# Sweeping the first weight pair of a sublayer by high and low parts, an earlier norm of half A, and x updates ahead of low parts

## The reference, cut to what matters

```python
def rmsnorm(x, g):
    y = xf * lax.rsqrt(jnp.mean(xf * xf, axis=-1, keepdims=True) + EPS)
    return (y * g.astype(jnp.float32)).astype(x.dtype)
def ffn_half(x, g_pre, g_post, w_gu, w_dn):
    return x + 0.5 * rmsnorm(swiglu(rmsnorm(x, g_pre), w_gu, w_dn), g_post)
...
    x = ffn_half(x, g[0], g[1], w_ffn_gu[l, 0], w_ffn_dn[l, 0])
    u = rmsnorm(x, g[2])      # u @ w_in, two attentions, then @ w_out
    x = x + rmsnorm(mix, g[3])
    qc = (rmsnorm(x, g[4]) @ w_cq[l])
    x = x + rmsnorm(oc, g[5])
    x = ffn_half(x, g[6], g[7], w_ffn_gu[l, 1], w_ffn_dn[l, 1])
```

## Time and profile before

| | us |
|---|---|
| median of 3 runs | 2788.9 (2785.92 to 2790.43) |
| the profiled execution, its own time | 2787.24 |
| its span, first to last instruction | 2785.4 |
| PE busy | 2610.1 (94%) |
| DVE busy | 1272.3 (46%) |
| ACT busy | 900.8 (32%) |

### The profile page before, as it was taken

The page is one execution under the profiler, slowest core; times in us unless marked ns, Lnnn a source line. Parts: engine busy times, 40 slices in busy tenths (PEclk is TensorE's granted clock), DMA queues, the critical chain, the costliest instruction groups (busy, mean ns, idle before and its releaser), DMA issues.

```text
span 2785.4 us, 48225 instructions
## 1 busy us (share of the span) xinstructions
PE 2610.1 (94%) x19513; PEld 2471.8 (89%) x19513; DVE 1272.3 (46%) x2307; ACT 900.8 (32%) x1576; POOL 67.9 (2%) x199
## 2 busy tenths in 40 slices
PE   7999998999898889999989999989898988999998
PEld 6999998986587789999989999989755977999998
DVE  4444325345846554442254442253457555444323
ACT  3222223224533432222232222232344534322221
POOL 1000000001100000000000000000111000000000
PEclk9999999999989999999999999999998998999999
DMA  5233332330023023233223233233310321223321
GB/s 178 85 88 90 91 91 86 116 120 25 24 91 105 18 68 90 84 95 94 67 69 88 85 92 93 73 101 116 105 40 31 92 75 31 83 83 90 97 84 64
DMA packets 383972, 229.81 MB, mean 83 GB/s; under 512 B 6636, under 2 KB 371198, under 8 KB 383840
## 3 DMA queue, kind: packets, MB, share of 16 engines
q1 hardware_dynamic: 378272, 206.59, 25.3%
q0 software_dynamic: 4368, 16.92, 1.7%
q10 hardware_dynamic: 1200, 4.46, 0.4%
HBM read 214.39 MB, written 18.79 MB: 84 GB/s over the span
## 4 chain that ended last, share of the span: by engine, by line
PE 83%; DVE 11%; ACT 2%; issue 2%; DMA 1%; DVEq 0%; SPq 0%; ACTq 0%
PE psum L607 73%; PE psum L810 3%; PE psum L582 3%; PE psum L829 2%; DVE u_lo L1280 2%; DVE w_lo L1285 2%; DVE x L1326 1%; DVE probs L1469 1%; PE psum L622 1%; DVE y_ffn L1320 1%; DVE y_mix L1320 1%; ACT w_hi L993 1%; PE psum L823 1%; PE psum L831 0%; DMA w_raw<-in_w_ffn_gu 0%
## 5 line engine op out<-in xcount | busy, mean ns | idle before, releaser
L607 PE MATMUL psum<-u_hi,w_hi 128*128 128x272 f32 x4096 | 906.8, 295 | 62.1 <-DVE w_lo L1285 24.2
L607 PE MATMUL psum<-u_hi,w_lo 128*128 128x272 f32 x4096 | 894.3, 292 | 0.0
L607 PE MATMUL psum<-u_lo,w_hi 128*128 128x272 f32 x4096 | 892.3, 292 | 0.0
L607 PEld LDWEIGHTS psum<-u_hi,w_hi 128*128 128x128 f32 x4096 | 671.7, 193 | 72.8 <-DVE u_lo L1280 28.3
L993 ACT ACTIVATE w_hi<-w_raw 128x1024 fp32r<-128x1024 f32 (+1 forms) x336 | 376.8, 1121 | 1105.6 <-PE psum L607 1091.2
L607 PEld LDWEIGHTS psum<-u_lo,w_hi 128*128 128x128 f32 x4096 | 672.5, 193 | 0.0
L607 PEld LDWEIGHTS psum<-u_hi,w_lo 128*128 128x128 f32 x4096 | 667.9, 193 | 0.0
L1285 DVE TENSOR_TENSOR w_lo<-w_raw,w_hi 128x1024 fp32r<-128x1024 f32 (+1 forms) x336 | 436.5, 1299 | 348.3 <-ACT w_hi L993 348.3
L607 PE MATMUL psum<-h_hi,w_hi 128*128 128x272 f32 x1408 | 305.7, 288 | 0.5
L607 PE MATMUL psum<-h_lo,w_hi 128*128 128x272 f32 x1408 | 304.5, 287 | 0.0
L607 PE MATMUL psum<-h_hi,w_lo 128*128 128x272 f32 x1408 | 304.4, 287 | 0.0
(11 more groups left out here) (189 smaller groups left out, 2097.1 us busy)
## 6 DMA issues: line engine op xcount, KB each, us to landing
w_raw<-in_w_ffn_gu SPq DMA_DIRECT2D x176, 512.0 KB, 3.8
w_raw<-in_w_ffn_dn SPq DMA_DIRECT2D x64, 704.0 KB, 4.6
w_raw<-in_w_in SPq DMA_DIRECT2D x48, 512.0 KB, 3.7
w_raw<-in_w_out SPq DMA_DIRECT2D x16, 512.0 KB, 3.9
w_raw<-in_w_ckv SPq DMA_DIRECT2D x16, 512.0 KB, 3.8
bias_tab_dram<-bias_rev_dram POOLq DMA_DIRECT2D x1, 5120.0 KB, 21.3
table<-bias_tab_dram SPq DMA_DIRECT2D x16, 320.0 KB, 2.9
out<-k_nat POOLq DMA_DIRECT2D x4, 1024.0 KB, 5.0
```

The costliest lines, as they stand in the source:

```text
L607: pe_last[0] = pe.matmul(psum[:, bank + part, 0:c1 - c0], w, xx[:, c0:c1], start=s0, stop=s1)
```

## The change

PE's `first_chunks` no longer runs the three products of a block together. It makes sweeps over all eight blocks with one kind of product: for half A, high x high and then high activation x low weight for slot 0, the same for slot 1 (with half B's spread of y between the two), then the low activations of slot 0 and of slot 1; for half B, slot 0's and slot 1's sweeps likewise, with the low activations of slot 0 ahead of slot 1's low weights. Each matmul of a sweep waits for its own block. In the last output tile of a feed-forward sublayer, half A's norm comes before the fifth of the eleven blocks of half B's first part (slot 0), and its spread before the ninth, both in the same part; before, the norm stood behind that part and the spread in the second. ACT makes slot 1's `w_hi` after the last two high parts of half A and not before them. DVE does all four y and x steps of a half and then the eight low parts, with slot 1's low weights after the fourth. `sum_x` is split: `fold_x` does its first addition, and `late_sums` puts the low weights between the fold and the rest.

Eight low parts stand there now between the two copies; before there were two. The diff, cut to its core:

```diff
-            half_chunk(pair, 0, 0, u_in, range(KD), 0, True, True, arrived(0))
-            if between:
-                between()
-            half_chunk(pair, 1, 2, u_in, range(KD), 0, True, True)
-            half_chunk(pair, 0, 0, u_in, range(KD), 1, True, True, arrived(1)).then_inc(chunk_done, 1)
-            half_chunk(pair, 1, 2, u_in, range(KD), 1, True, True).then_inc(chunk_done, 1)
+            def sweep(slot, bank, half, weight, part, first=False, last=False):
+                for k in range(KD):
+                    u = (u_hi, u_lo)[part]
+                    pe.wait_ge((u_hi_ready, u_lo_ready)[part], 16 * q + 8 * half + k + 1)
+                    if first and half == 0 and slot == 0 and k == 4 and norm_late:
+                        norm_late()
+                    pe_last[0] = pe.matmul(psum[:, bank + half, 0:H], weight[:, slot, k * 128:(k + 1) * 128],
+                                           u[:, k, half * H:half * H + H], start=first and k == 0, stop=last and k == KD - 1)
+                return pe_last[0]
+            pe.wait_ge(w_hi_ready, 2 * pair + 1)
+            sweep(0, 0, 0, w_hi, 0, first=True)
+            pe.wait_ge(w_lo_ready, 2 * pair + 1)
+            sweep(0, 0, 0, w_lo, 0)
+            pe.wait_ge(w_hi_ready, 2 * pair + 2)
+            sweep(1, 2, 0, w_hi, 0, first=True)
+            if spread_late:
+                spread_late()
+            pe.wait_ge(w_lo_ready, 2 * pair + 2)
+            sweep(1, 2, 0, w_lo, 0)
+            sweep(0, 0, 0, w_hi, 1, last=True)
+            sweep(1, 2, 0, w_hi, 1, last=True)
+            sweep(0, 0, 1, w_hi, 0, first=True)
+            sweep(0, 0, 1, w_lo, 0)
+            sweep(1, 2, 1, w_hi, 0, first=True)
+            sweep(0, 0, 1, w_hi, 1, last=True).then_inc(chunk_done, 1)
+            sweep(1, 2, 1, w_lo, 0)
+            sweep(1, 2, 1, w_hi, 1, last=True).then_inc(chunk_done, 1)
...
-            half_chunk(pair, 0, 2, h_in, range(DNB), 1, True, False).then_inc(chunk_done, 1)
-            norm_y(l, st, 0)
             def early(k):
-                if k == DNB + 5:
+                if k == 4:
+                    norm_y(l, st, 0)
+                if k == 8:
                     spread_y(l, st, 0)
-            half_chunk(pair, 1, 2, h_in, range(DNB, KF), 1, False, True, early).then_inc(chunk_done, 1)
+            half_chunk(pair, 0, 2, h_in, range(DNB), 1, True, False, early).then_inc(chunk_done, 1)
+            half_chunk(pair, 1, 2, h_in, range(DNB, KF), 1, False, True).then_inc(chunk_done, 1)
...
             root_late()
-            cut_second()
             for k in range(6, KD):
                 high(q, 0, k, gain)
+            cut_second()
...
-                if p and gain is not None:
-                    low(q, half, 2 * p - 2, gain)
-                    low(q, half, 2 * p - 1, gain)
...
-                low(q, half, KD - 2, gain)
-                low(q, half, KD - 1, gain)
+                for k in range(KD):
+                    low(q, half, k, gain)
+                    if later:
+                        later(k)
...
+            fold_x(q, 0)
+            cut_lo(pair + 1, 0)
             sum_x(q, 0)
-            cut_lo(pair + 1, 0)
+            fold_x(q, 1)
+            cut_lo(pair + 1, 1)
             sum_x(q, 1)
-            cut_lo(pair + 1, 1)
```

30 lines of the change are left out of this document (16 added, 14 removed).

## The result

| | before | after |
|---|---|---|
| median of the first 4 runs of each, us | 2787.41 (2784.29 to 2790.43) | 2768.33 (2765.27 to 2771.31) |
| the profiled execution, its own time | 2787.24 | 2765.27 |
| its span | 2785.4 | 2763.5 |
| granted clock over the span | 0.968 | 0.972 |

Five more runs gave 2768.44.

A forecast was written before the change was run, and what follows sets the result against it. PE bounds the kernel (busy 94% of the span), so only places where it waits or runs slowly count; 4.3 + 3.4 + 3.2 + 1.6 - 4.6 - 0.2 = 7.7 us gained, median 2781.2, range 2769.5 to 2789.

The forecast's parts named there:

- FFN handover: Handover where half B's update starts 5.8 us earlier and the tail behind it loses 1.5: 4.3 us gained.
- two IN handovers: Handovers timed to the next norm of x: gain 2.8 us, less 1.1 for another clock fall; 3.4 for two.
- two CO handovers: Handovers with half A's norm unmoved: half B starts 2.2 us earlier, the tail loses 0.6; 3.2 for two.
- end of the program: At the program's end, half B's update starts at 2766.5 instead of 2768.14, and the output follows: 1.6 us gained.
- in front of cross-attention, two: Ahead of cross-attention, DVE's block of eight low parts and waits for weights make PE 2.3 us later; 4.6 for two layers.
- long runs: Stretches of 2844 back-to-back matmuls, 357.75 us, 0.126 each: claimed unable to get shorter, so no gain counted.
- rival 1: In PE's sweeps, each met wait costs up to 0.10 us more per matmul, 488 matmuls, 49 us: 2830; chance 9%.
- what half B's start waits for: In IN and FFN handovers, DVE: PE's spread is done at 442.4, before DVE is free at 443.6; 5.8 us earlier.
- the tail at the lower clock: Behind half B's start, 24 matmuls at 0.227 us: next pair at +14.6, IN norm at +19.1 (full clock +12.3, +16.9).
- The charge of 1.1: In each IN handover, 1.1 us for the chance of another clock fall after PE's idle 2.3 us.
- rival 2: PE keeps its full clock through the handovers' sparse stretches: 19.4 us gained, 2769.5; chance 13%.
- rival 3: In the handovers the tail eats the head through more clock falls and later weights: 0.9 us gained, 2788; chance 18%.

The follow-up runs named there:

- after_all_fill: The changed kernel plus matmuls with unread results where PE idles in and behind handovers and ahead of the four long runs; 2769.74 us.
- early_norm_only: The kernel before with only half A's earlier norm and spread, at three handovers behind a feed-forward sublayer and at the end; 2775.31 us.

## Why the prediction was too small

The change gains 19.1 us by the medians and 21.0 by the two pairs of spans; the sum had 7.7 on six kinds of places. By the marks of two traces each:

| step of the prediction | forecast gain | measured |
|---|---|---|
| FFN handover | 4.3 | 5.5 |
| two IN handovers | 3.4 | 6.0 |
| two CO handovers | 3.2 | 5.2 |
| end of the program | 1.6 | 1.7 |
| in front of cross-attention, two | -4.6 | -4.7 |
| start | -0.2 | +1.9, mostly scatter |
| between the handovers | not in the sum | 5.4 (long runs 5.8) |

*Right.* The order of the marks in a handover: half A starts 3.0 earlier and half B 5.1 (forecast 5.8) in the IN and FFN handovers; half B of a CO handover starts 2.35 earlier (2.2). The end came out in size. So did the loss ahead of cross-attention with its cause, though PE starts 2.9 us later there and not 2.3, and what follows gives some of it back. A sweep's matmul costs 0.126 us with its own wait, so rival 1 falls. The page TensorE: Matmul & The Clock Gate of the Trainium skill (Step-by-step: what each phase is for) says that weight loads are pulled ahead of running matmuls; the rows now show that a wait already met leaves the spacing as it was.

*Wrong in part: what half B's start waits for.* The prediction put two sweeps at full clock, 2.0 us, ahead of the spread of y, and had it done before DVE was free. In the first IN handover the 16 matmuls take 3.3 us (436.06 to 439.34), at the lower level in part, and DVE waits 0.42 for the spread; in the six IN and FFN handovers of two traces it waits 0.24 to 0.51. The prediction named such a wait as a sign of being wrong; here it is small. That is most of the 0.7 missing in the head.

*Wrong, first step: the tail at the lower clock.* Of the 40 matmuls behind half B's last high part the prediction took all 24 up to the end of slot 0 at the lower level, and 1.1 us more in the IN handovers for a fall behind the idle time. From half B's start to `norm_x` that is +19.1, without the charge. The four IN handovers of the two traces measured 19.7, 18.3, 18.3 and 17.1. The full-clock end that the prediction named, 16.9, is real: after_all_fill, with its clock at 1.00, has 17.1 in both. But in three of the four the low level doesn't last for the 24 matmuls up to slot 0: it covers 6.8 us of the tail of 19.7, 3.4 us in each of 18.3, and nothing in that of 17.1. So the mean, 18.4, lies between the two ends, and the tail grew by 2.1 (from 16.3) and not by 3.0, while the head gained 0.7 less than forecast. The charge of 1.1 can't be in these marks, since the fall comes behind `norm_x`: three of the four places have one, 1.2 to 2.2 us behind its start, where one of four had it before, and the stretch from there to the next half-A sum takes 364.4 us against 363.6. So 0.8 of the charge is real and stands under "between". By the marks that is 1.3 more for each IN handover, 2.6 in all, of which 1.6 is paid back there. In a CO handover the tail was to lose 0.6 and gained 0.2 (19.2 to 19.0), which makes most of the 2.0 missing there. In the FFN handover it is the traces of before that differ, 41.0 and 43.2; against the first alone the gain is 4.4, as forecast.

The experiments show the same error from another side. The early norm moves half A by 3.0 us in three handovers and the end by 1.6; if half B follows, that is 10.6, and early_norm_only gained 12. A sum of 7.7 for the whole change therefore says that the sweeps and the new order lose 2.9 us. They gain 6.9 by the medians (2775.31 to 2768.4); by the marks 2.9 in the handovers, the loss ahead of cross-attention included, and 6.1 between them (2402.7 to 2396.6).

*Wrong, second step, and the largest term: the long runs, put at nothing.* The prediction read the earlier trace rows as a run that can't get shorter, 0.126 us a matmul. 357.75 / 2844 is that number, and it hides the 2 us at its beginning. The stretches' view of the earlier trace rows was asked only at the handovers. The first 6 us of a long run would have shown a clock below full and 35 matmuls where 48 fit. The change doesn't touch this wait, and in the mean gets 5.8 us there, 1.4 for each long run. That it gets them is luck: nothing in the change aims at the place of the wait, and no step of the prediction could have given the size, since whether a fall comes depends on where in time the wait lies. But rival 2 (2769.5, the clock keeps up) could have been widened by 4 x 1.4, to 2764, and then the range would have held the time. That rival 2's 2769.5 is so near the measured 2768.33 doesn't bear it out: the clock was 0.56 in the tail of the first handover.

Two sums of the prediction don't come out of their own terms: rival 3 gives 1.2 us and not 0.9, and the IN tail at full clock 16.6 and not 16.9, which puts rival 2 at 2768.9. The measured time lies below that too.

*A third point the result alone would have hidden.* The prediction priced the early norm and the new order as one, "half B 5.8 earlier". The experiments show them as unlike: the early norm alone gives 12 us, the sweeps and the order 5 on top of nothing and 7 on top of the early norm, and the sweeps without the order lose 20.

## What to carry to other kernels

Look for the instruction that starts a chain too late before reordering the chain: the norm that was moved by 21 matmuls gave more than everything else. Sweeping by operand moves a whole sweep behind the last block, so it belongs only where the last block is made early. And an average spacing over thousands of matmuls hides a slow start: read the granted clock of the first microseconds behind each wait of PE, and if it falls there, matmuls whose result nobody reads hold it up, as long as they stand only where PE is idle.
